# The adaLN rows of a decoder layer computed in four 32-column groups of the array

## The reference, cut to what matters

```
ada = silu(c) @ w_ada + b_ada            # (9, 1024) @ (1024, 6144)
sh1, sc1, gt1, sh2, sc2, gt2 = split(ada, 6)
h = rmsnorm(x, g_pre_mix) * (1 + sc1) + sh1
m = token_mixers(h)                      # gated DeltaNet and a convolution branch
x = x + gt1 * rmsnorm(m, g_post_mix)
h = rmsnorm(x, g_pre_ffn) * (1 + sc2) + sh2
x = x + gt2 * rmsnorm(moe(h), g_post_ffn)  # top 4 of 32 experts
```

## Time and profile before

| | |
|---|---|
| median of three runs | 1992.04 us |
| span of the profiled execution | 1987.6 us |
| mean granted clock of PE, share of full | 0.860 |
| matmuls of `rows`, 192 passes | 86.9 us in all |
| first stretch: first ada matmul to last columns | 9.28 to 47.9 us |
| second stretch: rows(4) to columns(11) | 343.75 to 444.5 us |

### The profile page before, as it was taken

How to read it: one execution, slowest core, us unless ns; L and a number is a source line. 1 busy time by engine, 2 the same in 40 slices (tenths; PEclk the granted TensorE clock), 3 DMA queues, 4 the chain that set the end, 5 groups by cost and what they waited for, 6 DMA issues and landing times.

```text
span 1987.6 us, 22944 instructions
## 1 busy us (share of the span) xinstructions
PE 1676.6 (84%) x7686; PEld 1346.4 (68%) x7686; DVE 1568.3 (79%) x1568; ACT 1018.2 (51%) x931; POOL 287.4 (14%) x275
## 2 busy tenths in 40 slices
PE   6999968998989689897988888888979888888880
PEld 1888857457866567676777776776767677767760
DVE  1462599496373689998999989999989999899975
ACT  1222401211311346766767767767667677677651
POOL 1000075271060000101001001000010010010104
PEclk9899978999889758888888897988888888979885
DMA  9645411362405528899898998998998989989934
GB/s 336 223 150 142 149 43 43 114 191 77 169 0 233 205 89 345 333 379 373 332 373 360 355 372 342 368 379 330 380 370 336 372 354 353 378 340 369 381 116 180
DMA packets 120891, 533.38 MB, mean 268 GB/s; under 512 B 10064, under 2 KB 10576, under 8 KB 86544
## 3 DMA queue, kind: packets, MB, share of 16 engines
q1 hardware_dynamic: 112992, 506.58, 66.0%
q0 software_dynamic: 6640, 21.89, 3.4%
q10 hardware_dynamic: 1216, 4.33, 0.6%
HBM read 508.23 MB, written 24.54 MB: 268 GB/s over the span
## 4 chain that ended last, share of the span: by engine, by line
PE 43%; issue 7%; DVE 6%; ACT 5%; DMA 1%; POOL 0%; DVEq 0%; ACTq 0%; POOLq 0%
PE ps L728 24%; PE ps L751 16%; ACT stH L1002 4%; PE ps L738 3%; DVE workL L1433 2%; DVE AS L1487 1%; DVE hT L1476 1%; ACT G L1018 1%; DVE hT L1477 0%; DMA ring<-yrows_dram,rowi 0%; DVE work L332 0%; DVE hT L1482 0%; DVE hT L1479 0%; DMA yrows_dram<-qT 0%; POOL ring L1630 0%
## 5 line engine op out<-in xcount | busy, mean ns | idle before, releaser
L1433 DVE TENSOR_TENSOR ringL<-ring,stH 128x2048 fp32r<-128x2048 f32 x264 | 586.2, 2281 | 1.8 <-ACT stH L1002 1.8
L1002 ACT ACTIVATE stH<-ring 128x2048 fp32r<-128x2048 f32 x264 | 492.5, 1911 | 19.3 <-PE ps L751 18.0
L728 PE MATMUL ps<-stH,XS 128*128 128x512 f32 x1056 | 414.8, 393 | 6.1 <-DVE ringL L1433 5.9
L728 PE MATMUL ps<-ringL,XS 128*128 128x512 f32 x1056 | 416.4, 394 | 0.0
L751 PE MATMUL ps<-stH,AS 128*128 128x512 f32 x528 | 255.6, 484 | 128.9 <-DVE AS L1487 128.9
L1433 DVE TENSOR_TENSOR workL<-work,stH 128x2048 fp32r<-128x2048 f32 x132 | 301.4, 2283 | 51.4 <-ACT stH L1002 51.4
L1002 ACT ACTIVATE stH<-work 128x2048 fp32r<-128x2048 f32 x132 | 250.7, 1899 | 0.0
L751 PE MATMUL ps<-workL,AS 128*128 128x512 f32 x528 | 246.4, 467 | 0.0
L426 PE MATMUL ps<-hT,ring 128*128 128x264 f32 x1024 | 240.7, 395 | 0.0
L751 PEld LDWEIGHTS ps<-stH,AS 128*128 128x128 f32 x528 | 126.6, 240 | 164.5 <-DVE workL L1433 131.8
L728 PEld LDWEIGHTS ps<-stH,XS 128*128 128x128 f32 x1056 | 198.6, 188 | 51.8 <-issue 5.9
(11 more groups left out here) (357 smaller groups left out, 1825.2 us busy)
## 6 DMA issues: line engine op xcount, KB each, us to landing
ring<-gate_up_dram SPq DMA_DIRECT2D x264, 1024.0 KB, 11.3
work<-down_dram SPq DMA_DIRECT2D x132, 1024.0 KB, 6.5
ring<-in_dram SPq DMA_DIRECT2D x16, 2048.0 KB, 11.1
ring<-ada_dram SPq DMA_DIRECT2D x12, 2048.0 KB, 8.6
yrows_dram<-qT POOLq DMA_DIRECT2D x33, 256.0 KB, 6.7
yrows_dram<-S SPq DMA_DIRECT2D x1, 4096.0 KB, 20.5
ring<-pw_dram SPq DMA_DIRECT2D x2, 2048.0 KB, 7.7
ring<-out_dram SPq DMA_DIRECT2D x2, 2048.0 KB, 8.2
```

Of the source, the lines that this page charges most:

```text
L728: mm = pe.matmul(bank(n), XS[:, i, :], part[:, n * 512:(n + 1) * 512], start=(i == 0 and a == 0), stop=(i == GU - 1 and a == 1))
L1002: act.activation(stH[:, i % NSTG, :], raw(i), ACT.Copy).then_inc(hi_done, 1)
L1433: dve.tensor_tensor(low(i), raw(i), stH[:, i % NSTG, :].bitcast(F32), ALU.subtract).then_inc(lo_done, 1)
```

## The change

The eight contraction tiles of an ada block are dealt to four column groups of the array: tile k goes to group k modulo 4, and its result goes to PSUM partitions 32q to 32q+31, q = k mod 4. Each group so sums two tiles. The stationary operand is widened from 9 to 32 columns; columns 9 to 31 of `cT` are set to zero by a new POOL instruction, for which PE waits once (`c_pad`). ACT copies all 128 partitions of the bank. The four transposes of `columns` become four plain matmuls over 128 partitions, with a new constant `fold9` of 9 columns as the moving operand: it has a one where the partition modulo 32 is the column, so the product adds the four partial sums while it turns rows into columns. `cT` is now stored 32 wide, and its load writes 9 of every 32 numbers of a partition; the constant tile `cv` is 9 columns wider. Two small tiles of the end are merged into one (`sums`), with the same use.

On every engine the instructions stand in the same order as before, but for the new one at the head of POOL's stream. Each `rows` still has eight matmuls, each `columns` four.

```
-        cT = sb("cT", [P, KD, 1 + NDE])
+        cT = sb("cT", [P, KD, QT])              # QT = 32
-        arow = misc[0:1 + NDE, :]
+        arow = misc[:, :]
...
-            sp.dma_start(cT[:, :, :], A["cT"]).then_inc(in_c, 16)
+            sp.dma_start(cT[:, :, 0:1 + NDE], A["cT"]).then_inc(in_c, 16)
...
                 for k in range(KD):
-                    mm = pe.matmul(ps[0:1 + NDE, a % 2, :], cT[:, k, :], ring[:, j % RING, k, :],
-                                   start=(k == 0), stop=(k == KD - 1))
+                    q = k % 4
+                    mm = pe.matmul(ps[QT * q:QT * (q + 1), a % 2, :], cT[:, k, :], ring[:, j % RING, k, :],
+                                   start=(k < 4), stop=(k >= KD - 4))
                 mm.then_inc(ada_rows, 1)
...
-                    tr = pe.transpose(ps[:, a % 2, (1 + NDE) * i:(1 + NDE) * (i + 1)],
-                                      arow[:, i * P:(i + 1) * P], ident[0:1 + NDE, 0:1 + NDE])
+                    tr = pe.matmul(ps[:, a % 2, (1 + NDE) * i:(1 + NDE) * (i + 1)], arow[:, i * P:(i + 1) * P],
+                                   con("fold9"), start=True, stop=True)
...
             pe.wait_ge(c_silu, 1)
+            pe.wait_ge(c_pad, 1)
...
-            act.activation(cT[:, :, :], cT[:, :, :], ACT.Silu).then_inc(c_silu, 1)
+            act.activation(cT[:, :, 0:1 + NDE], cT[:, :, 0:1 + NDE], ACT.Silu).then_inc(c_silu, 1)
...
-                act.activation(arow[:, :], ps[0:1 + NDE, a % 2, :], ACT.Copy).then_inc(ada_copied, 1)
+                act.activation(arow[:, :], ps[:, a % 2, :], ACT.Copy).then_inc(ada_copied, 1)
...
         def _(pool):
+            pool.memset(cT[:, :, 1 + NDE:], 0.0).then_inc(c_pad, 1)
             pool.memset(ones[:, :], 1.0)
...
+    put("fold9", i % QT == np.arange(1 + NDE)[None, :])
```

More of the change, by code:

```diff
@@ L58 @@
 RING = 4
+QT = 32
 PV = {}
@@ L70 @@
 _at = 0
-for _name, _n in (("ident", P), ("upper", P), ("levels", LEVELS * P), ("eps", 4)):
+for _name, _n in (("ident", P), ("upper", P), ("levels", LEVELS * P), ("eps", 4), ("fold9", 1 + NDE)):
     CV[_name] = (_at, _at + _n)
@@ L195, in build @@
         GT = cg[0:E, :, :, :].rearrange("e a k n -> e (a k n)")[:, 0:NT]
-        ss = sb("ss", [P, 3, 1])
-        rs = sb("rs", [P, 3, 1])
+        sums = sb("sums", [P, 2, 3, 1])
+        ss, rs = sums[:, 0, :, :], sums[:, 1, :, :]
         ps = ctx.enter_context(nc.psum_tensor("ps", [P, 8, 512], F32))
@@ L247, in build @@
         dve_chain, act_chain, pool_chain = sem("dve_chain"), sem("act_chain"), sem("pool_chain")
-        memset_done = sem("memset_done")
+        memset_done = sem("memset_done"); c_pad = sem("c_pad")
         ada_rows = sem("ada_rows"); ada_copied = sem("ada_copied")
```

## The result

The changed kernel takes 1956.12 us (median of four executions, 1953.60 to 1958.08), the kernel before beside it 1992.36 us: ratio 0.9821, 95% interval 0.9807 to 0.9835, so 36 us less and not the 17.2 that were forecast. The profiled execution of after has a span of 1956.4 us, 31.2 less than that of before.

The account below looks back on a forecast made before the run. It took PE's chain in two stretches before the untouched expert loop as what counts, with DVE bounding c = 1: 8.7 + 8.0 + 0.5 = 17.2 us, 1992.0 - 17.2 = 1974.8 us. Range 1969 to 1980; 8 in 10, 1967 to 1996.

Parts of the forecast that it names:

- What bounds the kernel: Whole kernel: PE holds 43% of the waits, nearly all in the untouched expert loop, so only two stretches before it count.
- The rows: Each ada block on PE: only neighbouring tiles' passes overlap, 9 steps for 16 passes, 3.86 us, saving 3.00 us; chance 0.48.
- all four groups stream together: Rival for the ada blocks: 1.72 us a block, 9.2 to 11.2 us and 11.8 us gained, about 1969 us; chance 0.22.
- First stretch: First four ada blocks up to ACT's last columns: end at 39.2 in place of 47.9 us, 8.7 us gained.
- bound by the transfer: Rival's first stretch, all four groups streaming: the fourth block's landing at 30.9 us sets rows(3), ending at 32.8; chance 0.22.
- half rate: Same rival, first stretch: PE, idle between blocks, may fall back to half rate, ending columns up to 2 us later.
- cT: Load at the start, now 1024 pieces of 36 bytes: delays the first ada block and x by 0.8 us.
- Columns: Four matmuls in place of transposes after a block: 0.8 to 0.85 us, adding 0.5 us a block, at most 1.2.
- End of c = 0: Second stretch: three rows 3.0 us shorter each, two columns 0.5 us longer each; 8.0 us gained.
- c = 1: Five more rows shorten by 3.0 us each, but DVE hides them; only 0.5 us counted.
- The sum: Whole kernel: 8.7 + 8.0 + 0.5 = 17.2 us off, giving 1974.8 us.

Follow-up runs that it names:

- e1: Memory layout of the changed kernel (wider cT and cv, merged small tiles) with the rows, copy and transposes of the kernel before; 1975.19 us, ratio 0.9925.
- e7: Kernel before with 9 unused columns in the constant tile and small tiles merged, moving all tiles behind by 32 bytes; 1976.62 us, ratio 0.9929.
- e14: Kernel before, padded so that stH, XS and AS lie on multiples of 64 bytes, G and all behind 32 bytes off; 1974.32 us, ratio 0.9922.
- e2: Changed kernel with neighbouring tiles 2q and 2q+1 in column group q, in place of k modulo 4; 1949.52 us, ratio 0.9798.
- e4: Changed kernel with one reciprocal of the second norm, ahead of the expert loop, done twice on DVE; 1950.77 us, ratio 0.9799.
- e13: Changed kernel with 29 of POOL's 31 convolution taps left out; 1903.13 us, ratio 0.9554.
- e9: Kernel before with 32 bytes of padding ahead of XS: stH stays 32 bytes off a multiple of 64, XS and all behind on one; 1988.93 us, ratio 0.9992.

## Why the prediction was wrong

*What bounds the kernel, wrong in one step, and the costliest.* "Nearly all in the expert loop, which the change does not touch. So only two stretches count": the loop stood at nothing. Its code is untouched, the addresses of its operands are not: 15.1 us come from there (e1, e7, e14). The change makes `cv` 9 columns wider, and the loop's tiles lie behind it; the prediction gave the wider tiles a cost as a transfer only. With them the forecast's own terms give 1992.0 - 17.2 - 15.1 = 1959.7.

*The rows, wrong step.* "So pass 2 of a tile can run beside pass 1 of the next tile, and not more: 9 steps", 3.86 us a block. Measured 1.92 us, four steps and a tail, in the order of the change and in that of e2 alike. The order that the passes keep on PE as a whole was taken as a bound on every group; the rule of the Trainium skill cited for it, "TensorE: Matmul & The Clock Gate", on packing small matmuls, is not borne out by these passes: in program order by tiles, after would need 9 steps a block and e2 13. The factor of up to 4 of the Trainium skill, "TensorEngine Tiling (Array Packing)", on key properties and speedup, agrees: 7.03 / 1.92 = 3.7. The rival "all four groups stream together" had this part right, block (1.72 and a tail) and stretch.

*First stretch, right by luck.* Forecast end 39.2 us, measured 39.36. The 2.7 us more at L459 cost nothing, because PE then waited for the fourth block. In all seven kernels with new first blocks it waits there, 1.1 to 2.4 us, and rows(3) starts at 31.0 to 31.3 us, whether L459 took 5.49 us (e4) or 6.73 (e2). The forecast had 31.4, just after the landing; the rival "bound by the transfer". In e2:

```profile
31.21 1.95 PE L439 MATMUL ps<-ring,cT 128*32 128x512 f32 x16 [1.08 <-DMA ring<-ada_dram]
```

Behind that the two errors cancel: rows(3) takes 2.5 us in place of 3.9, and from there to ACT's end it takes 5.9 in place of 3.9, as PE ran at the half rate that the rival had named (0.8 us more in each of two columns, 0.6 in rows(3)). From the start of rows(3) to the coefficients it takes 6.3 us in e2, nearly at the full rate, and 8.9 in e13, where rows(3) and both columns are slow. Over the 11 kernels with old first blocks and the 7 with new ones the coefficients start at 49.0 and 39.0 us on average: 10.0 us, within the rival's 9.2 to 11.2.

*cT, right.* 0.8 us of delay taken; its landing takes 2.8 us and not 2.0, and the first block starts at 10.14 and not 9.28.

*Columns.* 0.8 to 0.85 us forecast; measured 1.06 with the drain, 0.41 before. At the full clock ACT starts 0.64 us later behind them and PE's next product 0.56: near the 0.5 taken. At the half rate in the first stretch it is 0.8 us more.

*End of c = 0.* 8.0 us forecast. From coefficients to state copy it is 327.1 - 314.8 = 12.3 us where DVE's taps don't collide (the rival's 11.8; its cover by DVE's taps and scalings shows as 1.01 us of waiting at L563 and 0.80 at L574), and 6.5 us in the profile of after, where they do. That DVE could be longer "meeting POOL's taps at another moment" was foreseen for c = 1 only.

*c = 1, right.* From the state copy to the loop it takes 375.5 us before, 372.5 in after and 370.6 to 373.9 in kernels with old rows there; no gain can be told from none, as forecast (0.5 us). PE waits there for DVE, as the earlier trace rows had shown:

```profile
389.80 3.75 PE L538 MATMUL ps<-work 128*128 128x128 f32 x16 [8.73 <-DVE work L1197]
410.50 3.75 PE L538 MATMUL ps<-work 128*128 128x128 f32 x16 [10.21 <-DVE work L1202]
```

*The sum.* 10.0 us on average and 12.3 from the rows and 15.1 from the place, less 5.7 where the taps collide (320.5 - 314.8): 31.7 us, near the profiles' 31.2. That the profile's gain up to the loop, 18.0 us, comes near the forecast's 17.2 is luck: the rows gained more than forecast, and the collision took 5.7 of it. The medians say 36; single executions of one of these kernels lie 2 to 11 us apart. The range ended at 1967 because no case in it held a change in the operands of the loop.

**What stays open.** Why passes with only one operand on a multiple of 64 bytes are slower than with none in four of the five cases of the table (396 against 392 ns; those on XS in e9 are not) was not found, nor why `ringL` passes, whose operands in e9 both lie on such a multiple, are slow there (393 ns, 389 in e14) where those of `stH` stand between them. Passes of other types and shapes were not tried against the address. Which executions lose at the taps was not steered.

## What to carry to other kernels

Four float32 products with 32 columns of output or fewer can stream at once in column groups, in either of the two orders tried, and the sum over groups can go into the product that turns them. But what a shorter stretch leaves PE idle came back in part as the lower clock here, and the wait for the next block's transfer took its place as the bound. A change of tile sizes moves every tile behind it: compare the addresses of the operands of the hot loop modulo 64 before and after, and pad for it on purpose. Before a gain of a few microseconds is believed or explained, look whether two engines that exclude each other met differently in that execution.

## What the runs showed of the hardware

In the loop's F32R passes (128x128 stationary, 512 columns moving, one start every 227 ns), a moving operand, a stationary one or both 32 bytes off a multiple of 64 cost 3 to 8 ns a pass. Both off cost 15 us in this kernel's 33 rounds; e7, nine unused columns, gains that 0.7% without any change of the work. At the full clock passes of four column groups started 6 to 7 ns apart in after and 13 to 17 in e2, and the block took 1.92 and 1.94 us. A product of POOL over 1024 columns took 2.44 us where DVE's taps were held up and 5.48 where they ran through; 13 taps took 5.22 us by themselves and 12.7 beside POOL's.
